# Modulation rows moved by another engine, a reordered attention front, early rotary copies and single last rows in a two-block kernel

## What is computed

```
first_block:
  q,k,v,a,g = split(rms_norm(x) @ w_in)
  attn  = neighbourhood_attention(q, k, v, rpb)          # 8 heads of 64
  conv  = silu(layer_norm(depthwise_conv31(a*sigmoid(g))))
  x     = x + concat(rms_norm(attn), rms_norm(conv)) @ w_out
  x     = x + expert_choice_ffn(rms_norm(x))             # 16 experts, 32 tokens each
  x     = rms_norm(x) * final_g
second_block:
  mod   = silu(c) @ w_ada + b_ada, and the same for c_ctx # six rows of 1024 each
  h     = modulate(rmsnorm(x)); q,k,v,z,gl = split(h @ w_in)
  q,k   = axial_rope(q,k)                                # rotary positions
  y     = mix_branches(diff_attention(q, k_all, v_all), spatial_gating(gelu(z)), gl)
  x     = x + gt1 * rmsnorm(y @ w_out)
  h     = modulate(rmsnorm(x))
  x     = x + gt2 * rmsnorm(peer(h))
peer, per token t: 8 heads x 16 chosen rows; out[t] = sum gelu(h[t].u[row]) * gate * v[row]
```

## Time and profile before

| | us |
|---|---|
| median of three runs | 2171.39 |
| lowest and highest | 2169.92, 2172.47 |
| the profiled execution | 2167.82 |
| its span in the trace | 2166.0 |

### The profile page before, as it was taken

One profiled execution on the slowest core, in us unless ns is written; L12 is line 12 of the kernel. 1 busy time (PEld: TensorE's weight loads), 2 busy tenths in 40 slices (PEclk: granted clock), 3 DMA queues, 4 the chain that ended last, 5 costly groups with the idle time before them and its releaser, 6 DMA issues.

```text
span 2166.0 us, 24516 instructions
## 1 busy us (share of the span) xinstructions
PE 1473.2 (68%) x10272; PEld 605.4 (28%) x10272; DVE 743.6 (34%) x1856; ACT 430.1 (20%) x979; POOL 290.9 (13%) x265
## 2 busy tenths in 40 slices
PE   8988766766776656656568999996766644444344
PEld 7544311322221111111114445553345401000000
DVE  5823101000000000000003123426676776867764
ACT  1331110000000000000002164544245522222211
POOL 0000000000000000000000000003443444544441
PEclk9988978888897788887789999998878755555555
DMA  9568999999999999999995446669999999999996
GB/s 394 214 255 368 413 426 428 426 428 427 427 426 428 426 427 427 426 429 425 428 425 215 154 160 232 229 247 360 418 420 420 419 419 419 420 420 419 420 419 277
DMA packets 75582, 810.04 MB, mean 374 GB/s; under 512 B 8433, under 2 KB 8561, under 8 KB 9809
## 3 DMA queue, kind: packets, MB, share of 16 engines
q1 hardware_dynamic: 38416, 539.83, 60.0%
q0 software_dynamic: 36864, 268.45, 30.0%
q10 hardware_dynamic: 192, 0.20, 0.0%
HBM read 807.20 MB, written 1.05 MB: 373 GB/s over the span
## 4 chain that ended last, share of the span: by engine, by line
DMA 48%; PE 31%; DVE 13%; issue 3%; POOL 2%; ACT 2%; ACTq 0%; DVEq 0%; POOLq 0%
DMA AR<-in_w_down 18%; DMA AR<-in_w_up 16%; PE PS L380 14%; DMA AR<-in_peer_uv,AR 14%; DVE AR L1375 3%; PE PS L607 3%; PE PS L628 2%; POOL AR L1754 2%; PE PS L391 2%; PE PS L495 1%; DVE AR L891 1%; PE PS L814 1%; PE PS L771 1%; DVE AR L893 1%; PE PS L707 1%
## 5 line engine op out<-in xcount | busy, mean ns | idle before, releaser
L1754 POOL DMA_INDIRECT AR<-in_peer_uv,AR x256 | 289.1, 1129 | 1668.1 <-DVE AR L1366 1358.8
L607 PE MATMUL PS<-AR 128*32 128x512 f32 x2048 | 304.3, 731 | 185.6 <-DMA AR<-in_w_up 128.7
L814 PE MATMUL PS<-AR 32*32 32x512 f32 x4096 | 231.1, 941 | 289.7 <-ACT AR L1714 289.7
L1375 DVE CUSTOM_DVE_ANT_0 AR<-AR 128x1024 f32<-128x1024 f32 x256 | 309.1, 1223 | 153.4 <-DMA AR<-in_peer_uv,AR 152.9
L380 PE MATMUL PS<-AR 128*128 128x512 f32 x736 | 329.4, 603 | 6.3 <-ACT AR L1435 2.9
L628 PE MATMUL PS<-AR 128*32 128x512 f32 x1024 | 172.4, 809 | 104.0 <-DMA AR<-in_w_down 97.9
L1065 DVE TENSOR_TENSOR AR<-AR,PS 128x512 f32<-128x512 f32 x16 | 11.0, 688 | 591.9 <-PE PS L607 591.9
L380 PEld LDWEIGHTS PS<-AR 128*128 128x128 f32 x736 | 139.4, 193 | 177.0 <-issue 176.4
L607 PEld LDWEIGHTS PS<-AR 128*32 128x32 f32 x2048 | 62.6, 122 | 416.9 <-DMA AR<-in_w_up 206.5
L814 PEld LDWEIGHTS PS<-AR 32*32 32x32 f32 x4096 | 39.3, 127 | 445.3 <-ACT AR L1714 437.1
L1079 DVE COPY AR<-PS 128x512 f32<-128x512 f32 x16 | 11.1, 692 | 283.1 <-PE PS L628 283.1
(11 more groups left out here) (273 smaller groups left out, 1229.6 us busy)
## 6 DMA issues: line engine op xcount, KB each, us to landing
AR<-in_w_gate SPq DMA_DIRECT2D x64, 2048.0 KB, 26.2
AR<-in_w_up SPq DMA_DIRECT2D x64, 2048.0 KB, 25.8
AR<-in_w_down SPq DMA_DIRECT2D x64, 2048.0 KB, 26.2
AR<-in_w_in SPq DMA_DIRECT2D x29, 2048.0 KB, 7.9
AR<-in_w_ada SPq DMA_DIRECT2D x12, 2048.0 KB, 10.8
AR<-in_w_out SPq DMA_DIRECT2D x6, 2048.0 KB, 9.7
AR<-in_peer_w_query SPq DMA_DIRECT2D x6, 2048.0 KB, 10.8
AR<-in_w_branch_sgu SPq DMA_DIRECT2D x4, 2048.0 KB, 7.6
```

Of the source, the lines that this page charges most:

```text
L607: x = pe.matmul(PS[32 * q:32 * q + 32, bk, :], XS[:, j, e * 32:(e + 1) * 32], IN[key][:, jj, q * 512:(q + 1) * 512], start=(j == 0), stop= ...
L814: x = pe.matmul(PS[c:c + 32, ACC[a][g], :], DI[t, p, r, :], AR[t, off + 1024 + m * 512:off + 1536 + m * 512], start=(h == 0 and p == 0), s ...
L1375: v.tensor_tensor_reduce(rows, rows, HB[:, a, :], 1.0, 0.0, MULT, ADD, DOT[:, ix, k:k + 1]).then_inc(*w.hit("dot", ix, k))
L1754: pool.indirect_dma_start(out=AR[:, off:off + 2048], out_offset=None, in_=D["peer_uv_2"], in_offset=bass.IndirectOffsetOnAxis(ap=EI[:, ix, ...
```

## The change

Four things are changed.

1. ScalarE's `ada(p)` only copies. Six row buffers (ROWBUF) take the pieces: MR for p = 0, 2, 4, the two halves of XN for 1 and 3, a part of HT for 5. GpSimd issues the moves in a new `ada_rows(p)`, pieces 0 to 3 before its wait for `x1 0 1 1`, 4 and 5 behind it. The copy waits for the moves of p-2 only for p = 2 and 4; the squares of h2, which write XN, wait for pieces 1 and 3.
2. The front's order: `softmax(2)` and `softmax(3)` follow each other on ScalarE, and `ada(1)` comes ahead of them; `ada(2)` moves behind `scores(3)`; `out_half` now does one tile `a` at a call, and `out_half(1, 0)`, `values(2)`, `turn_p(3)`, `out_half(1, 1)`, `values(3)`, `ada(3)` follow in this order. VectorE's gain of the convolution (`conv_gain`) comes behind `softmax(2)`, the reciprocal of its norm behind `softmax(3)`.
3. In ORDER a stage `raw` stands directly behind each `kq`; ScalarE's raw copy is taken there.
4. Rows 12 to 15 of the last head are taken one by one: ScalarE scales a full 128x128 diagonal (LAST, made by VectorE in `rt5(15)`), and TensorE adds it with two full 128x512 products into the two final banks. The four banks of all the rows before are folded into the same two banks between rows 13 and 14. For the first tile the order stays.

```diff
-            todo = [("norm_turn", 0), ("kq", "k", 0, 0), ("norm_turn", 1), ("kq", "k", 0, 1), ("rope", "k", 0, 0)]
-            held = ("rope", "k", 0, 1)
-            for x, n in (("k", 1), ("q", 0), ("q", 1)):
-                for a in range(2):
-                    todo += [("kq", x, n, a), held]
+            todo = [("norm_turn", 0), ("kq", "k", 0, 0), ("raw", "k", 0, 0), ("norm_turn", 1)]
+            held = ("rope", "k", 0, 0)
+            for x, n in (("k", 0), ("k", 1), ("q", 0), ("q", 1)):
+                for a in range(x == "k" and n == 0, 2):
+                    todo += [("kq", x, n, a), ("raw", x, n, a), held]
                     held = ("rope", x, n, a)
...
-                if n and n % 2 == 0:
+                if n and n % 2 == 0 and n < 254:
                     todo.append(("v", *divmod(n // 2 - 1, 8)))
...
-                if k % 2:
+                if 252 <= n < 256:
+                    todo.append(("last", k))
+                elif k % 2:
                     todo.append(("act", ix, k // 2))
+                if n == 253:
+                    todo.append(("part", 1))
...
             turn_p(1)
             ada(1)
-            ada(2)
             values(1)
             conv_stat()
             scores(3)
+            ada(2)
             turn_p(2)
-            out_half(1, ("cmt",))
+            out_half(1, 0, ("cmt",))
             values(2)
             turn_p(3)
+            out_half(1, 1)
+            values(3)
             ada(3)
-            values(3)
...
+            def last_row(k):
+                off, _ = ROWS[15, k]
...
+                for m in range(2):
+                    x = pe.matmul(PS[:, banks.at("leave", 1, m), :], LAST[:, k - 12, :], AR[:, off + 1024 + m * 512:off + 1536 + m * 512],
+                                  start=(k == 12), stop=(k == 15), skip_group_check=True)
...
             values(0)
             conv_var()
             softmax(2)
+            conv_gain()
             values(1)
             conv_stat()
             softmax(3)
-            for a in range(2):
-                out_half(1, a, ssc, "conv")
+            rstd2("conv", ssc)
+            out_half(1, 0, ssc, "conv")
             values(2)
+            out_half(1, 1, ssc, "conv")
...
+                if ix == 15:
+                    for k in range(12, 16):
+                        v.tensor_scalar(LAST[:, k - 12, :], ident, GT[:, ix, k:k + 1], None, MULT).then_inc(*w.hit("gated_row", k))
...
                     w.wait_ge("mm", "mr", p, half)
-                    if p:
-                        w.wait_ge("mr_row", p - 1)
-                    act.copy(cut, PS[:, banks.at("mr", p, half), :]).then_inc(*w.hit("mr", p, half))
-                    w.wait_ge("mr", p, half)
-                    for i in range(2):
-                        r = 64 * half + 8 * p + 4 * i
-                        act.dma_start(CR[r:r + 4, :], cut[i::32, :]).then_inc(
-                            *w.hit("mr_row", *((p,) if half + i == 2 else (p, half, i)), by=16))
+                    if p in (2, 4):
+                        w.wait_ge("mr_row", p - 2)
+                    act.copy(ROWBUF[p][:, half * 512:(half + 1) * 512], PS[:, banks.at("mr", p, half), :]).then_inc(*w.hit("mr", p, half))
...
+            turn_p(1)
             w.wait_ge("cnorm")
...
             act.activation(SQ, DW, ACT.Square).then_inc(*w.hit("csq2"))
+            ada(1)
             softmax(2)
-            turn_p(1)
-            ada(1)
+            softmax(3)
+            turn_p(2)
             ada(2)
             root("conv", ssc)
-            softmax(3)
-            turn_p(2)
             turn_p(3)
...
                 w.wait_ge("x1", 0, 1, a)
+                w.wait_ge("mr_row", 2 * a + 1)
                 row_square("h2", a, ss2[:, a:a + 1])
...
+            def last_row(k):
+                one = WT[:, 15, k:k + 1]
+                w.wait_ge("dot", 15, k)
+                w.step(act.activation(one, DOT[:, 15, k:k + 1], ACT.Gelu))
+                w.wait_ge("gated_row", k)
+                w.wait_step()
+                act.activation(LAST[:, k - 12, :], LAST[:, k - 12, :], ACT.Copy, scale=one).then_inc(*w.hit("last", k))
...
+            def ada_rows(p):
+                for half in range(2):
+                    w.wait_ge("mr", p, half)
+                    for i in range(2):
+                        r = 64 * half + 8 * p + 4 * i
+                        pool.dma_start(CR[r:r + 4, :], ROWBUF[p][i::32, half * 512:(half + 1) * 512]).then_inc(
+                            *w.hit(f"mr_row{p}", half, i, also=[("mr_row", p)] if half + i == 2 else (), by=16))
+
+            for p in range(4):
+                ada_rows(p)
             w.wait_ge("x1", 0, 1, 1)
```

More of the change, by code:

```diff
@@ L483, in conv_stat, with out_half @@
                 x.then_inc(*w.hit("mm", "css"))
-            def out_half(q, *after):
+            def out_half(q, a, *after):
                 key = ("w_out", q)
-                for a in range(2):
-                    for n in range(2):
-                        b, before = banks.use("x1", q, n, a)
-                        w.wait_ge(*before)
-                        w.wait_ge("in", *key)
-                        for event in after:
-                            w.wait_ge(*event)
-                        for j in range(4):
-                            x = pe.matmul(PS[:, b, :], MT[:, 4 * q + j, a * 128:(a + 1) * 128], IN[key][:, j, n * 512:(n + 1) * 512],
-                                          start=(j == 0), stop=(j == 3))
-                        x.then_inc(*w.hit("mm", "x1", q, n, a, also=[("used", *key)] if n + a == 2 else ()))
+                for n in range(2):
+                    b, before = banks.use("x1", q, n, a)
+                    w.wait_ge(*before)
+                    w.wait_ge("in", *key)
+                    for event in after:
+                        w.wait_ge(*event)
+                    for j in range(4):
+                        x = pe.matmul(PS[:, b, :], MT[:, 4 * q + j, a * 128:(a + 1) * 128], IN[key][:, j, n * 512:(n + 1) * 512],
+                                      start=(j == 0), stop=(j == 3))
+                    x.then_inc(*w.hit("mm", "x1", q, n, a, also=[("used", *key)] if n + a == 2 else ()))
             banks.ids = list(range(7))
@@ L528, in tensor @@
                 x.then_inc(*w.hit("mm", "amt", a))
-            out_half(0, ("amt", 0), ("amt", 1))
+            for a in range(2):
+                out_half(0, a, ("amt", 0), ("amt", 1))
             lg, lg_before = banks.use("lg")
@@ L831, in tensor @@
                     "gain2p": lambda: row_of("g2"), "ht": heads_turn, "ba": ba, "yt": y_turn, "op": op, "ft": ffn_turn, "take": take,
-                    "qm": qm, "qs": qs, "rt0": rt0, "back": back, "v": v_step, "leave": leave}
+                    "qm": qm, "qs": qs, "rt0": rt0, "back": back, "v": v_step, "part": fold_parts, "last": last_row}
             for stage, *x in ORDER:
@@ L1415, in vector @@
                     "norm_turn": norm_turn,
[L1416 removed]
+                    "fte": ffn_turn, "qse": query_mean, "rt1": rt1, "rt2": rt2, "rt3": rt3, "rt4": rt4, "row": row, "rt5": rt5, "part": part, "leave": leave}
             for stage, *x in ORDER:
@@ L1715, in weights, with part @@
                 i.then_inc(*w.hit("diag", ix, p))
+            def last_row(k):
[5 more added lines that the diff above has]
+                act.activation(LAST[:, k - 12, :], LAST[:, k - 12, :], ACT.Copy, scale=one).then_inc(*w.hit("last", k))
+            def part(a):
+                w.wait_ge("mm", "row", 8 * a + 7, 5 if a else 7)
+                for g in (0, 2):
+                    act.copy(PART[:, g, :], PS[:, ACC[a][g], :]).then_inc(*w.hit("part_a", a, g, also=[("part", a, g)]))
             def leave(a):
@@ L1720, in leave @@
                     act.activation(SMX[:, 0, 3:4], ones[:, 0:1], ACT.Sqrt)
-                w.wait_ge("mm", "row", 8 * a + 7, 7)
-                for g in (0, 2):
-                    act.copy(PART[:, g, :], PS[:, ACC[a][g], :]).then_inc(*w.hit("part_a", a, g, also=[("part", a, g)]))
                 for m in range(2):
@@ L1733, in scalar @@
                     "up1": lambda a: root(("y2", a), ss5[:, a:a + 1]), "up2": up2, "fn1": lambda a: root(("x5", a), ss6[:, a:a + 1]),
-                    "fte": ffn_turn, "qme": qm, "qse": lambda h, a: root(("q", 8 * a + h), RQ[:, a, 2 * h:2 * h + 2]), "rt4": rt4, "bke": back, "act": weights, "leave": leave}
+                    "fte": ffn_turn, "qme": qm, "qse": lambda h, a: root(("q", 8 * a + h), RQ[:, a, 2 * h:2 * h + 2]), "rt4": rt4, "bke": back, "act": weights, "last": last_row, "part": part, "leave": leave}
             for stage, *x in ORDER:
```

47 lines of the change are left out of this document (30 added, 17 removed).

## The result

The changed kernel takes 2151.28 us (median of four runs, 2149.43 to 2153.10); the kernel before, run beside it, 2170.65 (2168.25 to 2172.47). The ratio is 0.9911, with a 95% interval of 0.9897 to 0.9924. In a later group of runs the same two kernels gave 2148.20 and 2170.43, ratio 0.9889 (0.9874 to 0.9904). The forecast was 2150.4.

What follows compares the result with a forecast made beforehand. TensorE and its waits bound the front and mixer, DMA the expert stage and the last row's landing. Gains of 12.3 + 5.4 + 3.3 = 21.0 us off the 2171.39 median gave 2150.4 us, range 2145 to 2160.

Steps and rivals of the forecast that it cites:

- Front: Stretch up to out_half(0): TensorE's new order without waits starts out_half(0) at 140.3, not 152.6; gain 12.3 us, between 9 and 14.2.
- the 15.67 that I kept: Front: out_half(0) was assumed to take 15.67 us, as before, its first 3.6 us having run at half clock.
- the 1.9 named as the upper end: Front: out_half(0) at full clock would take 13.8 us, 1.9 less, a gain left out of the 12.3.
- the 7.40 us in the chain: Front: ScalarE waits 7.40 us for ada(1)'s row moves before overwriting MR for ada(2), holding up TensorE's turn_p(2) transposes.
- Row moves on GpSimd: Front: GpSimd's moves taken to land in 7.40 us like ScalarE's, within 15.6 us of slack, so costing nothing.
- rows late: Rival, front: moves land like the gathers' median, giving back 4.7 us, 2155.1; with their maximum 2163.1; chance 0.10.
- slower than before: Rival, front: piece 3 lands over 36.6 us after issue and the h2 square waits; at 45 us 2179.8; chance 0.05.
- Mixer: Around the first vals: early raw copy removes TensorE's 3.57 us hole, slow transposes and slow restart; gain 5.4 us.
- TensorE is full from there on to the first gathers, so the gain is carried: Mixer: the 5.4 us gain was to persist to the first gathers, whose first issue it moves.
- End: Last rows: clock returns to full under unbroken full products, rows 12 to 15 and fold end sooner; gain 3.3, from -3.3 to 3.9.
- tail stays at half clock: Rival, end: the last rows run at half clock throughout; 14.4 us saved in all, 2157.0; chance 0.12.
- the rivals: Tail at half clock 0.12, rows late 0.10, half of the front lost 0.11, slower 0.05; the forecast itself 0.62.

Runs made afterwards that it cites:

- rows_only: Kernel before with only the six row buffers and GpSimd's row moves, all engines in the old order; 2162.74 us, ratio 0.9960.
- order_only: Kernel before with only the front's new order, one row buffer and ScalarE's row moves kept; 2159.42 us, ratio 0.9950.
- ada2_later: Kernel before with only ada(2) moved: behind scores(3) on TensorE, behind softmax(3) and turn_p(2) on ScalarE; 2172.08 us, ratio 1.0004.
- raw_on_before: Kernel before with only the early raw copies in ORDER; 2165.92 us, ratio 0.9974.
- front_only: Changed kernel without points 3 and 4 (early raw copies, single last rows), against the kernel before; 2158.31 us, ratio 0.9937.
- tail_on_before: Kernel before with only rows 12 to 15 of the last head taken singly and the early fold; 2168.50 us, ratio 0.9982.
- change_again: The changed kernel unaltered, run again in a later group against the kernel before; 2148.20 us, ratio 0.9889.
- one_buffer_gpsimd: The whole change but with one row buffer, GpSimd still issuing the moves, against the kernel before; 2149.13 us, ratio 0.9899.
- no_gpsimd: The whole change but with one row buffer and ScalarE issuing the row moves, against the kernel before; 2150.80 us, ratio 0.9905.

## Why the prediction was right, point by point

**Front: the sum right, its explanation wrong in part.** Forecast 12.3, measured 12.97 by the marks and 13.0 alone. `out_half(0)` was to start 39.8 us behind the end of `scores(2)`; it started 40.9 behind it (102.57 to 143.45). The terms that were off: `scores(3)` and `ada(2)` at a reduced clock, 2.7 more together; `conv_stat`, transposes and values somewhat cheaper than priced. In return `out_half(0)` took 13.99 and not the 15.67 that I kept, the 1.9 named as the upper end. So two errors of the clock's place cancelled. What failed is the step on the cause. The prediction said that ROWBUF takes the wait off, after naming the 7.40 us in the chain as what stops TensorE. In the old order that holds, with GpSimd's moves: `rows_only` gains 5.9 of the 7.40. But `order_only` shows that in the new order there is no such wait left to take off, and `ada2_later` that the 7.40 can go and nothing be gained, where the way in which they go uncovers another wait. The sum came out because it was not made from the wait: it added TensorE's own work in the new order and then asked of each helper whether it would be late. Had I subtracted 7.40 from the old chain, I would have been 5.6 us off.

**Row moves on GpSimd.** Taken at nothing, with ScalarE's landing of 7.40; they landed in 5.6 to 8.4, median 6.7, and nobody waited. In `rows_only`, where eight are issued in a row, the last took 10.7. The gathers' 20.3 of the earlier trace rows, the price of "rows late" and, drawn out, of "slower than before", was the wrong neighbour: those are 1 MB each and queue behind one another. The Trainium skill ("DMA: Bandwidth & Descriptors", "Issuing engine by pattern") gives simple loads and stores to SyncE and calls the path of SyncE and ScalarE generally faster. Here the last move of a piece landed after 6.8 to 8.4 us from GpSimd and 6.9 to 7.4 from ScalarE (by the copies that waited for it), under a DMA share of 0.97 to 1.01, and the front was 1.1 us shorter with the issues off a busy ScalarE. By the fixed cost of about 2 us that the same page gives for GpSimd's path ("Anatomy of one DMA — SWDGE (gpsimd) path") the moves should land sooner than they did; the measurement decides.

**Mixer: the net right, two terms missed.** Forecast 5.4, measured alone 5.6. The traces show how it is made up. From the last down product to the first gather the seven kernels without the early raw copies take 332.5 to 333.5 us, and six of the seven with them 325.6 (the seventh has its down product at half clock): 7.0 less, not 5.4. From the first gather to the dot of row 12 the seven without take 673.4 to 673.8, the seven with 674.8 to 675.5: 1.5 to 2 us given back. "TensorE is full from there on to the first gathers, so the gain is carried" was right as far as it went; that the row stage behind would pay was not seen. Laid over one another at the first gather, the traces of a kernel show where. Three stretches of 10 us, 20, 40 and 90 us behind it, first of `order_only`, which has the old copies, then of `raw_on_before`:

```profile
1481.33:1491.33 10.00, 3.70 (x68) 0.87 (x67) 9.13 (x37) 7.67 (x14) 3.46 (x4) 0.71 0.96 351
1501.33:1511.33 10.00, 8.39 (x74) 2.88 (x75) 9.93 (x18) 2.27 (x10) 6.31 (x4) 0.77 0.83 312
1551.33:1561.33 10.00, 10.00 (x83) 3.93 (x81) 4.21 (x7) 1.42 (x5) 5.45 (x4) 1.00 1.01 415
```

```profile
1487.33:1497.33 10.00, 4.58 (x68) 0.92 (x68) 9.12 (x37) 7.67 (x14) 3.74 (x4) 0.56 0.96 349
1507.33:1517.33 10.00, 8.39 (x71) 2.91 (x72) 9.93 (x18) 2.28 (x10) 6.31 (x4) 0.57 0.81 301
1557.33:1567.33 10.00, 10.00 (x83) 4.07 (x82) 4.19 (x9) 1.42 (x5) 3.68 (x3) 1.00 0.91 348
```

The work is the same, the clock is not: 0.56 and 0.57 where it was 0.71 and 0.77. In both, GpSimd's gathers wait for TensorE's products, which free the row buffers; in the third stretch it issues three gathers and not four, and the DMA share is 0.91 and not 1.01. The changed kernel repeats this (0.57, 0.56, share 0.94), the kernel before has the pattern of `order_only` (0.70, 0.77, share 1.01). So the clock's falls lie otherwise against the row stage wherever the early copies are in; how the copies do it, 260 us further on, is open. Of the 7.0, some 1.4 is the first product group behind the experts: 8.5 to 8.65 in the traces with the copies, 10.0 to 10.2 in six without them but 8.55 in `front_only`; that the copies bring it about is not shown.

**End.** Forecast 3.3; from row 12's dot to the end of the span 3.85 in the changed kernel, 3.29 in `tail_on_before`, and in `change_again` 2.16. The clock came back, as claimed, under full products without a gap; the rival "tail stays at half clock" is out. From row 12's first product to the last one the prediction had 10.6 to 11.9 us; it took 10.6 in the changed kernel, 11.1 in `tail_on_before` and 12.0 in `change_again`. The last product was to end 5.9 us behind the last dot's start; it ended 4.5 behind it, also because that dot was 0.8 us late: row 14 landed late. This is no work of VectorE's copies, since VectorE was idle for 0.88 us behind them, and in `one_buffer_gpsimd` the dot that follows the same copies comes 2.44 us behind the one before. Why the row landed late is open; it cost nothing, as TensorE was still busy. How much the end gains hangs on when the clock returns. `change_again`, chain of waits:

```profile
2131.96 6.54 PE PS L852 x8
```

**What lay outside the sum.** The start is 2.10 longer in the changed kernel's trace and the expert stage 1.60. The first is no work of the change: the first 64 products of L399 (L391 before) take 14.1 us or 15.7 to 16.3, in traces of old and new fronts alike. Nor is the second: four other traces with the old order of the front (`rows_only`, `raw_on_before`, `tail_on_before`, `ada2_later`) have 972.1 to 972.2 there, the six others with the new one and the old `ada(4)` 970.1 to 971.2; it is the profiled execution of before that was short, with 969.40. So the profiled pair understates the change, by 2.7 us there (972.1 less 969.4) and by 2.1 in the first products: 18.4 would be 23.2, where the medians gave 19.4 and 22.2.

**The chances.** None of the rivals came true, and the measured median lies 0.9 us above the forecast. That is closer than the method deserves: terms of 1 to 2 us were off in either direction, and the runs of one kernel spread by 4 us, in `no_gpsimd` by 7.6. That they cancelled is luck.

## What to carry to other kernels

A wait in the chain is not a price: the same 7.40 us were worth 5.9 removed in one way and nothing in another. Before counting a wait as a gain, lay the bounding engine's own work end to end in the new order and ask of every helper when it is ready, since what stands behind the wait may be late as well, and moving a step may uncover the wait that it had been filling. When a change brings new buffers, a new engine and a new order at once, try each alone; here the order did 11.9 of the 13.0 us in the front, and buffers and GpSimd without it 5.9. Where a gain seems carried to the end, compare the stages behind it too: of the mixer's 7.0 us the row stage took 1.5 to 2 back.

## What the runs showed of the hardware that I had not expected

At the start of the profile the clock column says full where the products are not at full speed. Two stretches, before and after:

```profile
14.00:16.00 2.00, 1.91 (x9) 1.74 (x10) 0.00 (x0) 0.00 (x0) 0.00 (x0) 1.00 1.00 426
```

```profile
14.00:16.00 2.00, 1.53 (x4) 1.29 (x5) 0.32 (x1) 0.00 (x0) 0.00 (x0) 1.00 1.04 442
```

Both have 1.00, but nine 128x256 products start in one and four in the other. The trace's first clock record begins at 13.1 us before and at 18.0 after, and where there is no record the column says 1.00. Over the 14 traces this first group of 64 takes 14.1 us in the five whose first record begins between 13.0 and 13.8, and 15.7 to 16.3 in the nine where it begins between 17.5 and 19.1. So it is the clock here too, and these 2 us are a part of the spread between runs. GpSimd issues a plain move in 563 ns, ScalarE in 503, and an 8 KB move inside SBUF lands in 5.6 to 8.4 us beside a full weight stream (10.7 for the last of eight in a row). And the mean clock was 0.59 between 112 and 118 us though TensorE had had no idle time since 97.8; before the fall it had done transposes, the products of `ada(1)`, and those of `values(1)` and `conv_stat`, 64 columns and one column wide. By the clock records it falls between 109.2 and 110.4 us in all nine traces with the new order.
